# Last gates ahead of last rows, residual on VectorE, first mixer re-dealt, and unread identity products on TensorE

## The chip, the cores and the metric

The kernel runs on one core of one Trainium2 chip. The metric is the device time of one execution in microseconds (us), from the host's side of the launch to its end; the traces give the span from the first to the last instruction. All engines work at once and meet through semaphores: TensorE (PE in the rows, its weight loads PEld), VectorE (DVE), ScalarE (ACT), GpSimd (POOL) and SyncE (SP), which issues the weight transfers.

## What is computed

Two blocks of two layers each, on 256 tokens of 1024 values in fp32. In each layer a swiglu feed-forward (FFN) stands on either side of a mixer. Block 1 normalises by root mean square, and its mixer has four branches, merged by gates; block 2 normalises by mean and variance after each part, and its mixer has two branches.

```python
# block 1, one layer
f = swiglu(rms_norm(h, g0), w_gate, w_up, w_down)      # 1024 -> 2816 -> 1024
h = h + 0.5 * rms_norm(f, g0_post)
a.., b.., c_q, c_k, c_v, d_q, d_k, d_v, d_f, gates = split(rms_norm(h, g1) @ w_in)
y_a = short_conv(...) @ w;  y_b = conv_31_layernorm_silu(...) @ w
y_c = rms_norm(differential_attention(c_q, c_k, c_v)) @ w
y_d = forgetting_attention(d_q, d_k, d_v, d_f) @ w
h = h + rms_norm((g_a*y_a + g_b*y_b + g_c*y_c + g_d*y_d) @ w_o, g1_post)
# then a second FFN like the first
# block 2, one layer (DN = 4 ** 0.25)
x = layernorm(DN * x + 0.5 * swiglu_2(x, w13, w2), g, b)
qa, ka, va, qkv_b, beta, dt, z, gates = split(x @ w_in)
y_a = sliding_window_attention(qa, ka, va, bias, sink) @ w_branch_a      # 16 heads
q, k, v = split(silu(conv_4(qkv_b)))
y_b = (rms(gated_delta_rule(l2(q), l2(k), v, g(dt), beta)) * silu(z)) @ w_branch_b   # 8 heads
x = layernorm(DN * x + (g_a * y_a + g_b * y_b) @ w_out, g, b)
# then a second FFN like the first
```

## The kernel before

**Products.** Every weight matrix comes from `stream` in units of up to 1 MB, by SP's queue, into a ring of four slots (`weight_ring`). ACT rounds a unit to a high part (L1537) and VectorE takes the low part as the difference (L1862); in block 2's mixer GpSimd takes it (L908) for the units of projections and gates. Each product of weights is then three products of parts on TensorE (high by high, low by high, high by low).

**Order.** `plan_first` and `plan_second` write a list of steps for one layer of each block, and every engine walks the same list and runs its own handler of each step, so the list is the order on every queue. A step that uses a weight unit draws in the splits of units that come later, ahead of its own work. `plan_ffn` deals an FFN: 22 steps `gu` (TensorE L1044, gate and up for 128 hidden values, whose silu is ACT's L1578 and whose split into parts VectorE's L1869 and L1871) and 11 steps `down` (L1101, of which each reads the hidden values of two `gu`). `interleave` weaves a chain of small dependent steps (attention, delta rule) into rounds of dense projection work and pops the steps that follow a finished projection from the list `later`, one for each step of the chain.

**Ends of the parts.** After the last rows (`last_rows`, L1112) ACT sums squares (block 1, `post`, L1585) or VectorE takes statistics (block 2, `post2`, L2150 to L2161), GpSimd computes the reciprocal root (L865, L867), and VectorE builds a diagonal (L1856) or the normed rows (L2161). TensorE then turns the rows for the next part (`xt`: L1061, fp32 products with the diagonal, in block 1; L1063, transposes, in block 2) into the PSUM banks 6, 7, 4 and 5. The sum of an FFN stands in the banks 0 to 3, that of a mixer in 4 to 7; VectorE reads bank 6, which holds the second half of the tokens, as the third of the four (L1939 or L2150).

**Mixer of block 1.** The chain is attention c (L1242 scores, L1257 turns, L1286 values), then its `out_norm`: squares by ACT (L1671), the root by GpSimd (L865, L867), the scaling by VectorE (L2105); then `out_turn`, and attention d. The gates are TensorE's L1346 with L1349 for the branch value, merged by VectorE's L2126.

**Mixer of block 2.** `pk`, `ps`, `pq` and `pv` project keys, small logits, queries and values. `cumg` (VectorE L2203, ACT L1746) sums the decays. For the eight heads of the delta rule `dtr` (TensorE L1402) turns queries and keys after the convolution (VectorE `taps` L2230 and L2232, `silu` L2245), `ddc` (L1428) and `dkk` build the decay matrix, and steps `dl0` to `du4` and `dot` solve two heads at a time. `affine` (GpSimd L935 and L937, in each of the three parts of a layer) makes the residual from the normed rows by gain and bias, four operations of 1024 columns.

## Time and profile before

| | |
|---|---|
| median of 3 runs | 3339.35 us (3338.19 to 3339.7) |
| profiled execution | 3333.8 us, span 3332.1 us, mean granted TensorE clock 0.959 |
| TensorE busy | 3070.4 us (92%) |
| VectorE, ScalarE, GpSimd busy | 1944.3, 1341.5, 532.0 us |
| block 1: FFN, mixer, FFN of layer 0 | 15 to 213, 219 to 572, 578 to 774 us |
| block 2: FFN, mixer, FFN of layer 0 | 1549 to 1770, 1772 to 2239, 2242 to 2441 us |

Layer 1 of each block repeats the pattern (784 to 1541 and 2446 to 3318 us). A row of the trace has the start in us, the duration in us (for several instructions from the first's start to the last's end), the engine, the line, the operation with its tiles, and in brackets the idle time of the engine ahead of it with what ended it. A row of the windows gives for a stretch the busy time of each engine with the count of its instructions, and then PEclk, the TensorE clock that was granted as a share of full speed: 1.00 is 2.4 GHz and 0.50 is 1.2 GHz.

### The profile page before, as it was taken

The numbers are of one execution on the slowest core, as the hardware profiler recorded it, in microseconds if no ns is written. First come the engines' busy times: TensorE is split into PE (matmuls) and PEld (weight loads), VectorE is DVE, ScalarE is ACT, GpSimd is POOL, SyncE is SP. The second block draws the span as 40 slices with busy tenths as digits, with TensorE's granted clock in tenths as the row PEclk, the third lists the DMA queues.
The fourth block names the chain that finished last, engine by engine and source line by source line (L and its number), as shares of the span: only waits on it lengthen the run. The fifth ranks groups of instructions, "written<-read, shape, count | busy, mean of one in ns | idle before, by whom it ended". The sixth has DMA issues, their size and how long they took to land.

```text
span 3332.1 us, 59102 instructions
## 1 busy us (share of the span) xinstructions
PE 3070.4 (92%) x22178; PEld 2901.9 (87%) x22178; DVE 1944.3 (58%) x3310; ACT 1341.5 (40%) x2224; POOL 532.0 (16%) x471
## 2 busy tenths in 40 slices
PE   8989999998989999998898978989989998889998
PEld 7989898998989999897797877989979888789897
DVE  4556776555556876554554576466565536654755
ACT  4344454434344454432333534434333345433332
POOL 0000000000000000001103444431010044444300
PEclk9999999999999999998898999999999989999999
DMA  5544444554544445456552321255545422123453
GB/s 207 182 159 153 132 144 168 176 188 148 189 158 154 142 142 171 165 186 150 198 202 102 102 77 54 87 177 181 190 162 200 160 100 89 64 66 138 170 188 127
DMA packets 72442, 495.49 MB, mean 149 GB/s; under 512 B 8064, under 2 KB 8240, under 8 KB 20176
## 3 DMA queue, kind: packets, MB, share of 16 engines
q1 hardware_dynamic: 67824, 471.95, 41.5%
q0 software_dynamic: 4048, 18.59, 2.1%
q8 instruction: 184, 3.01, 0.4%
q14 instruction: 114, 0.93, 0.1%
q10 hardware_dynamic: 272, 0.99, 0.1%
HBM read 487.31 MB, written 4.19 MB: 148 GB/s over the span
## 4 chain that ended last, share of the span: by engine, by line
issue 74%; PE 12%; DVE 6%; POOL 4%; POOLq 2%; DVEq 2%; ACT 1%; DMA 0%; ACTq 0%; SPq 0%
PE psum L1132 4%; POOL weights_low L908 2%; DVE work L2232 1%; PE psum L1346 1%; PE psum L1352 1%; POOL small L867 1%; POOLq L936 1%; PE psum L1242 1%; POOL residual L937 1%; POOLq L866 1%; DVE small L2257 0%; PE psum L1188 0%; DVE work L2318 0%; PE psum L1457 0%; DVEq L2235 0%
## 5 line engine op out<-in xcount | busy, mean ns | idle before, releaser
L1537 ACT ACTIVATE weights_high<-weight_ring 128x2048 fp32r<-128x2048 f32 (+3 forms) x788 | 906.8, 1171 | 1105.0 <-DMA weight_ring<-stream 1097.6
L1862 DVE TENSOR_TENSOR weights_low<-weight_ring,weights_high 128x2048 fp32r<-128x2048 f32 (+6 forms) x532 | 906.6, 1710 | 757.3 <-ACT weights_high L1537 753.8
L1044 PE MATMUL psum<-normed_t_high,weights_high 128*128 128x256 f32 x2816 | 802.5, 285 | 11.6 <-DVE normed_t_low L1871 10.5
L1044 PE MATMUL psum<-normed_t_low,weights_high 128*128 128x256 f32 x2816 | 800.2, 284 | 0.0
L1044 PE MATMUL psum<-normed_t_high,weights_low 128*128 128x256 f32 x2816 | 799.6, 284 | 0.0
L1044 PEld LDWEIGHTS psum<-normed_t_high,weights_high 128*128 128x128 f32 x2816 | 542.9, 193 | 17.4 <-DVE normed_t_low L1871 11.8
L1044 PEld LDWEIGHTS psum<-normed_t_low,weights_high 128*128 128x128 f32 x2816 | 543.9, 193 | 3.6
L1044 PEld LDWEIGHTS psum<-normed_t_high,weights_low 128*128 128x128 f32 x2816 | 543.6, 193 | 0.0
L1101 PE MATMUL psum<-weights_high,work_parts 128*128 128x512 f32 x1472 | 464.5, 397 | 19.5 <-DVE work_parts L1871 19.5
L1132 PE MATMUL psum<-normed_t_high,weights_high 128*128 128x256 f32 x1248 | 394.8, 316 | 3.2 <-DVE normed_t_low L1871 2.1
L908 POOL TENSOR_TENSOR weights_low<-weight_ring,weights_high 128x512 fp32r<-128x512 f32 (+1 forms) x216 | 346.2, 1618 | 274.6 <-ACT weights_high L1537 274.6
L1132 PE MATMUL psum<-normed_t_low,weights_high 128*128 128x256 f32 x1248 | 361.3, 290 | 0.0
L1132 PE MATMUL psum<-normed_t_high,weights_low 128*128 128x256 f32 x1248 | 360.7, 289 | 0.0
L865 POOL TENSOR_TENSOR small<-small 128x1 f32<-128x1 f32 (+3 forms) x74 | 18.9, 256 | 2107.5 <-ACT work L1585 992.6
L1101 PEld LDWEIGHTS psum<-weights_high,work_parts 128*128 128x128 f32 x1472 | 271.0, 189 | 77.8 <-DVE work_parts L1871 19.9
L1101 PE MATMUL psum<-weights_low,work_parts 128*128 128x512 f32 x736 | 290.9, 395 | 0.0
L1132 PEld LDWEIGHTS psum<-normed_t_high,weights_high 128*128 128x128 f32 x1248 | 248.0, 199 | 17.4 <-issue 11.3
L1346 PE MATMUL psum<-normed_t_high,weights_high 128*128 128x256 f32 x768 | 236.5, 308 | 14.8 <-DVE weights_low L1862 9.4
L1132 PEld LDWEIGHTS psum<-normed_t_low,weights_high 128*128 128x128 f32 x1248 | 248.5, 199 | 1.1
L1132 PEld LDWEIGHTS psum<-normed_t_high,weights_low 128*128 128x128 f32 x1248 | 247.0, 198 | 0.0
L1346 PE MATMUL psum<-normed_t_low,weights_high 128*128 128x256 f32 x768 | 222.5, 290 | 0.0
L1346 PE MATMUL psum<-normed_t_high,weights_low 128*128 128x256 f32 x768 | 222.2, 289 | 0.0
(268 smaller groups left out, 4477.5 us busy)
## 6 DMA issues: line engine op xcount, KB each, us to landing
weight_ring<-stream SPq DMA_DIRECT2D x400, 1024.0 KB, 4.9
weight_ring<-stream SPq DMA_DIRECT2D x64, 768.0 KB, 4.2
feature_rows<-feat POOLq DMA_DIRECT2D x6, 1024.0 KB, 5.1
work<-toeplitz_rows POOLq DMA_DIRECT2D x8, 512.0 KB, 6.6
feature_rows<-feat POOLq DMA_DIRECT2D x6, 512.0 KB, 3.8
toeplitz_rows<-work POOLq DMA_DIRECT2D x1, 3072.0 KB, 36.4
params<-prms POOLq DMA_DIRECT2D x5, 251.5 KB, 3.3
residual<-x SPq DMA_DIRECT2D x2, 512.0 KB, 4.3
```

Of the source, the lines that this page charges most:

```text
L866: pool.drain()
L867: pool.tensor_tensor(dst, dst, HALFNEG[:, 0:dst.shape[1]], ALU.pow).then_inc(signal, 1)
L908: pool.tensor_tensor(some(LOW, i, q, n), some(RING, i, q, n), some(HIGH, i, q, n).bitcast(F32), ALU.subtract).then_inc(low_by_pool, n)
L936: pool.drain()
L937: pool.tensor_tensor(H[:, t, :], H[:, t, :], PG[:, 1, :], ALU.add).then_inc(residual_ready, 1)
L1044: ins = pe.matmul(PS[:, bank, at:at + S], w[a][:, first + k, c * P:(c + 1) * P], src[b][:, k, :], start=(k, m) == (0, 0), stop=(k, m) == ( ...
L1101: ins = pe.matmul(PS[:, b, :], src[c][:, r, t * P:(t + 1) * P], w[a][:, r, n * HALF:(n + 1) * HALF], start=start and m == 0, stop=False, s ...
L1132: ins = pe.matmul(PS[:, job.bank, c * S:(c + 1) * S], w[i][:, k, c * P:(c + 1) * P], XT[j][:, k, :], start=(k, m) == (0, 0), stop=(k, m) = ...
L1242: ins = pe.matmul(dst, q[:, t * P:(t + 1) * P], k[:, 0:keys], start=True, stop=not extra, skip_group_check=True)
L1346: ins = pe.matmul(PS[:, job.bank, 0:S], w[p][:, r, 0:P], XT[q][:, r, :], start=(r, m) == (0, 0), stop=(r, m) == (KB - 1, 2), skip_group_ch ...
L1537: return act.activation(dst, src, ACT.Copy, scale=scale)
L1862: dve.tensor_tensor(some(LOW, i, q, n), some(RING, i, q, n), some(HIGH, i, q, n).bitcast(F32), ALU.subtract).then_inc(low_by_vector, n)
```

## The change

- `plan_ffn`: the last `gu` step goes ahead of the next-to-last `down`, so the end is gu20, gu21, down9, down10 where it was gu20, down9, gu21, down10. All eight FFNs.
- Ends of both mixers: before, the eight last gates and the rows steps ran 24 25, 26 27, wo0, 28 29, wo1, 30 31, wo2, wo3; now 24 to 27, 28 29, wo0, 30 31, wo1, wo2, wo3 (block 2: gates 0 to 7 likewise).
- Mixer of block 1: a step `out_square` (squares and root) follows attention c at once; the scaling comes three chain steps later and the turn after one more. The projections `dv` move behind those of branch a.
- Block 2: `affine` goes from GpSimd to VectorE, in four quarters of two operations of 512 columns, at gu4, gu6, gu8, gu10 of an FFN and after `pk`, the two `pq` and `pv` of a mixer. `feature` (the load of gains on GpSimd's queue) comes at gu12. `post2` drops its wait for the residual, and VectorE waits once for GpSimd's memsets ahead of block 2.
- Mixer of block 2: `cumg` moves into the attention; `taps` becomes single steps of one tap, and `interleave` pops two steps where more than four stand in `later`; the order in `prepare` changes; the scaling of `du4` becomes a step `dsc`; gates shift between the pairs of heads, so that the last pair has three dense units instead of four.
- `warm`: ahead of each wait for normed rows in `xt`, except at a layer's first `xt`, TensorE multiplies the identity by itself (fp32, 128 x 128) into the last quarter of the first `xt` bank: 24 and 4 products in block 1, 12 and 8 in block 2. Nothing reads them. The wait for the first bank stands ahead of them.

```diff
+WARM = {1: (24, 4), 2: (12, 8)}
...
@@ -178,11 +179,12 @@
     for j in range(FB):
         pl.step("gu", ("gu", s, j), banks=["hi"], s=s, j=j, unit=("gu", s, j),
                 signals=[("gate_silu_ready", 1), ("hidden_ready", 1)])
-        if j >= 2 and j % 2 == 0:
+        if 2 <= j < FB - 2 and j % 2 == 0:
             down(j // 2 - 1)
         for kind, signals, args in after:
             if j in args["j"]:
                 pl.step(kind, signals=signals, s=s, j=j, p=args["j"].index(j))
+    down(FP - 2)
     down(FP - 1)
...
         f()
-        if later:
-            later.pop(0)()
+        for _ in range(2 if len(later) > 4 else 1):
+            if later:
+                later.pop(0)()
...
-    chain.append((3, lambda: pl.step("out_norm", ("on", "c"), br="c",
-                                     signals=[("out_squares_summed", 1), ("out_rsqrt_ready", 1)])))
-    chain.append((2, out_turn("c")))
+    squares = (1, lambda: pl.step("out_square", "out_square",
+                                  signals=[("out_squares_summed", 1), ("out_rsqrt_ready", 1)]))
+    out_norm = (1, lambda: pl.step("out_norm", ("on", "c"), br="c"))
...
-    chain += chain_d[:8]
+    chain += [squares] + chain_d[:2] + [out_norm] + chain_d[2:3] + [(2, out_turn("c"))] + chain_d[3:8]
...
-    chain += [(2, lambda: pl.step("out_norm", ("on", "d"), br="d",
-                                  signals=[("out_squares_summed", 0), ("out_rsqrt_ready", 0)])),
-              (2, out_turn("d"))]
-    dense = [(16, lambda what=what, p=p: project(what, p)) for what in ("dq", "dk", "dv") for p in range(2)]
+    chain += [(2, lambda: pl.step("out_norm", ("on", "d"), br="d")), (2, out_turn("d"))]
+    dense = [(16, lambda what=what, p=p: project(what, p)) for what in ("dq", "dk") for p in range(2)]
     dense += [(16, lambda p=p: gate_a(p)) for p in range(4)] + [(16, lambda p=p: value_a(p)) for p in range(2)]
+    dense += [(16, lambda p=p: project("dv", p)) for p in range(2)]
     dense += [(12, lambda j=j: gate(j)) for j in range(24)]
     interleave(pl, chain, dense)
-    pl.steps += [gate(24)[0], gate(25)[0]]
+    pl.steps += [gate(j)[0] for j in range(24, 28)]
     acc = pl.step("acc", ("acc", 1), banks=acc_hi, s=1)
-    for k in range(2, KB + 1, 2):
-        if k < KB:
-            pl.steps += [gate(24 + k)[0], gate(24 + k + 1)[0]]
-        pl.step("wo", ("wo", k // 2 - 1), k=k // 2 - 1, unit=("wo", k // 2 - 1), src=("gy", 24 + k - 2))
+
+    def wo(k):
+        pl.step("wo", ("wo", k), k=k, unit=("wo", k), src=("gy", 24 + 2 * k))
+
+    pl.steps += [gate(j)[0] for j in range(28, 30)]
+    wo(0)
+    pl.steps += [gate(j)[0] for j in range(30, 32)]
+    for k in range(1, 4):
+        wo(k)
...
-        pl.step("affine", ("affine", s), s=s, signals=[("residual_ready", 2)])
         if s == 2:
             pl.step("params", signals=[("params_loaded", 16)])
-        if s != 1:
-            pl.step("feature", signals=[("feature_rows_loaded", 16)], s=s)
-        else:
+        if s == 1:
             pl.step("small_split", signals=[("small_weights_ready", 1)])
             pl.step("factors")
+
+    def affine(s, p):
+        pl.step("affine", s=s, p=p, signals=[("residual_ready", 1)])
 
     def post(s, acc):
         pl.step("post2", ("post", s), s=s, acc=acc,
@@ -375,7 +382,11 @@
     def ffn(s):
         begin(s)
         acc = pl.step("acc", ("acc", s), banks=acc_lo, s=s)
-        plan_ffn(pl, s, [("bias", [("bias_loaded", 16)], {"j": (3, 7, 11, 15)})] if s == 0 else [])
+        beside = [("affine", [("residual_ready", 1)], {"j": (4, 6, 8, 10)}),
+                  ("feature", [("feature_rows_loaded", 16)], {"j": (12,)})]
+        if s == 0:
+            beside.append(("bias", [("bias_loaded", 16)], {"j": (3, 7, 11, 15)}))
+        plan_ffn(pl, s, beside)
...
-        return host, [lambda: pl.step("taps", ("taps", hp, w, 0), hp=hp, w=w, p=0,
...
+        rest = []
+        for c in range(2):
+            for n in range(3):
+                rest.append(lambda c=c, n=n: pl.step("tap", hp=hp, w=w, p=c, a=n))
+            rest.append(lambda c=c: pl.step("taps", ("taps", hp, w, c), hp=hp, w=w, p=c, a=3,
+                                            signals=[("conv_ready", 1), ("conv_tanh_ready", 1)]))
+        rest.append(lambda: pl.step("silu", ("silu", hp, w), hp=hp, w=w, signals=[("conv_silu_ready", 1)]))
+        return host, rest
...
     pl.step("pk", "pk", banks=["lo"], unit=("w", 4))
+    affine(1, 0)
     pl.step("ps", "ps", banks=["lo"],
             signals=[("small_proj_ready", 1), ("small_logs_ready", 1), ("log_decay_ready", 1)])
     for p in range(2):
         pl.steps.append(query(p)[0])
+        affine(1, 1 + p)
     pl.step("pv", "pv", banks=["lo"], unit=("w", 5))
-    pl.step("cumg", "cumg", banks=["s"],
-            signals=[("decay_diff_ready", 1), ("decay_exps_ready", 1), ("decay_scalars_ready", 1)])
+    affine(1, 3)
...
+        for h, b in zip(hs, banks):
+            add(h, "dtr", b, [("qk_squares_summed", 1), ("qk_rsqrt_ready", 1)])
+            add(h, "dte", [], [("head_scalars_ready", 1)])
+        for h, b in zip(hs, banks):
+            add(h, "ddc", [3], [("decay_ready", 1), ("strict_decay_ready", 1)])
+            add(h, "dtf", b)
+        for h in hs:
+            add(h, "dkk", [3], [("level_masked", 1)])
+        return steps
...
+        for h in hs:
+            steps.append(lambda h=h: pl.step("dsc", ("dsc", h), h=h))
...
+    steps.insert(9, (2, lambda: pl.step("cumg", "cumg", banks=["s"],
+                                        signals=[("decay_diff_ready", 1), ("decay_exps_ready", 1),
+                                                 ("decay_scalars_ready", 1)])))
+    first = [(4, f) for f in prepare((0, 1), ((6, 7), (4, 5)))]
+    chain = steps + first[:1] + last + first[1:]
     dense = [(16, lambda p=p: query(p)) for p in (2, 3)] + [(16, lambda w=w: conv(0, w)) for w in range(3)]
     dense += [(16, lambda p=p: gated(p)) for p in range(2)] + [(16, lambda w=w: conv(1, w)) for w in range(3)]
+    dense += [(16, lambda: gate(0, 0, "lo3"))]
     interleave(pl, chain, dense)
...
-    extra = [[(16, lambda: gate(0, 0, "lo3"))] + [(16, lambda w=w: conv(2, w)) for w in range(3)],
-             [(16, lambda: gate(0, 1, "lo3"))] + [(16, lambda w=w: conv(3, w)) for w in range(3)],
-             [(16, lambda p=p: gated(p)) for p in (2, 3)] + [(16, lambda k=k: gate(0, k, "lo3")) for k in (2, 3)],
-             [(16, lambda k=k: gate(0, k, "lo3")) for k in range(4, 8)]]
+    extra = [[(16, lambda w=w: conv(2, w)) for w in range(3)] + [(16, lambda: gate(0, 1, "lo3"))],
+             [(16, lambda w=w: conv(3, w)) for w in range(3)] + [(16, lambda: gated(2))],
+             [(16, lambda: gated(3))] + [(16, lambda k=k: gate(0, k, "lo3")) for k in range(2, 5)],
+             [(16, lambda k=k: gate(0, k, "lo3")) for k in range(5, 8)]]
     for hp in range(pairs):
         chain = [(2, f) for f in solve((2 * hp, 2 * hp + 1))]
         if hp + 1 < pairs:
-            todo = [f for h in (2 * hp + 2, 2 * hp + 3) for f in prepare(h, (6, 7, 3))]
-            for n, f in enumerate(todo):
-                chain.insert(2 + 3 * n, (2, f))
+            todo = [(2, f) for f in prepare((2 * hp + 2, 2 * hp + 3), ((6, 7), (6, 7)))]
+            ends = chain[-4:]
+            chain = chain[:-4]
+            for n, item in enumerate(todo[:8]):
+                chain.insert(2 + 4 * n, item)
+            chain += todo[8:] + ends
         interleave(pl, chain, extra[hp])
...
+    pl.steps += [gate(1, k)[0] for k in range(4)]
...
+            def warm(bank, n):
+
+                for _ in range(n):
+                    pe.matmul(PS[:, bank, HALF - P:HALF], IDENT, IDENT, start=True, stop=True, skip_group_check=True)
+
             def xt(st):
                 flush()
 
                 n = named(("norm", st.s)).at["normed_ready"] if now.blk == 1 else 2 * st.s
-                for t in range(T):
+                first = st.jobs[0]
+                pe.wait_ge(bank_taken[first.bank], turn_at(first))
+                for t in range(T):
+                    warm(first.bank, WARM[now.blk][t] if st.s else 0)
                     pe.wait_ge(normed_ready, reach("normed_ready", n - 1 + t))
                     for k in range(KB):
                         job = st.jobs[k // 2]
-                        if t == 0 and k % 2 == 0:
+                        if t == 0 and k and k % 2 == 0:
...
+            def affine(st):
+
+                if st.p == 0:
+                    dve.wait_ge(feature_rows_loaded, reach("feature_rows_loaded", 16 * st.s))
+                t, cols = st.p // 2, slice(st.p % 2 * HALF, (st.p % 2 + 1) * HALF)
+                dve.tensor_tensor(H[:, t, cols], XN[:, t, cols], PG[:, 0, cols], ALU.mult)
+                dve.drain()
+                dve.tensor_tensor(H[:, t, cols], H[:, t, cols], PG[:, 1, cols], ALU.add).then_inc(residual_ready, 1)
+                dve.drain()
...
                 def stats(t, n):
                     job = st.acc.jobs[2 * t + n]
                     cols = slice(n * HALF, (n + 1) * HALF)
-                    if n == 0:
-                        dve.wait_ge(residual_ready, reach("residual_ready", 2 * (st.s + 1) - 1 + t))
...
             dve.tensor_copy(XN[:, :, :], H[:, :, :]).then_inc(normed_ready, T)
+            dve.wait_ge(zeros_set, 3)
```

How the order of instructions moves at three places. TensorE between the last rows of the first FFN of block 1 and the turn of the normed rows (line numbers of each kernel; `constants` is the identity), before:

```order
L1112 MATMUL psum<-weights_low,work_parts 128x512
L1054 REGISTER_ALU
L1058 REGISTER_ALU
L1061 MATMUL psum<-work,residual 128x128 x4
L1058 REGISTER_ALU
L1061 MATMUL psum<-work,residual 128x128 x2
```

And now:

```order
L1138 MATMUL psum<-weights_low,work_parts 128x512
L1077 REGISTER_ALU
L1070 MATMUL psum<-constants 128x128 x24
L1080 REGISTER_ALU
L1087 MATMUL psum<-work,residual 128x128 x4
L1084 REGISTER_ALU
L1087 MATMUL psum<-work,residual 128x128 x2
```

Twenty-four products of the identity stand between the last rows and the first turn; four more (L1070 x4) stand between the two halves of the tokens.

VectorE in the mixer of block 1 about the scaling of attention c (L2105, L2129 after), with the taps of branch b (L1979, L2003) and the gate's merge (L2126, L2150), before:

```order
L2126 SCALAR_TENSOR_TENSOR work<-work,psum 128x256
L2105 TENSOR_TENSOR work<-psum,small 128x512 x2
L1861 REGISTER_ALU
L1862 TENSOR_TENSOR weights_low<-weight_ring,weights_high 128x768
L2124 REGISTER_ALU
L2126 SCALAR_TENSOR_TENSOR work<-work,psum 128x256
```

And now:

```order
L2150 SCALAR_TENSOR_TENSOR work<-work,psum 128x256
L2003 SCALAR_TENSOR_TENSOR work<-work 128x232 x2
L1885 REGISTER_ALU
L1886 TENSOR_TENSOR weights_low<-weight_ring,weights_high 128x768
L2129 TENSOR_TENSOR work<-psum,small 128x512 x2
L1885 REGISTER_ALU
L1886 TENSOR_TENSOR weights_low<-weight_ring,weights_high 128x384
```

The scaling now stands behind a pair of taps and a low split, some 37 instructions of VectorE later in the layer.

VectorE in the mixer of block 2 at the first convolution (`taps`; L2230 and L2232 are L2264 and L2265 after), before:

```order
L2230 TENSOR_SCALAR work<-psum,params 128x256
L2232 SCALAR_TENSOR_TENSOR work<-psum,params,work 128x255
L2232 SCALAR_TENSOR_TENSOR work<-psum,params,work 128x254
L2232 SCALAR_TENSOR_TENSOR work<-psum,params,work 128x253
L2230 TENSOR_SCALAR work<-psum,params 128x256
L2232 SCALAR_TENSOR_TENSOR work<-psum,params,work 128x255
```

And now, at the second:

```order
L2264 TENSOR_SCALAR work<-psum,params 128x256
L2265 SCALAR_TENSOR_TENSOR work<-psum,params,work 128x255
L2110 REGISTER_ALU
L2113 REGISTER_ALU
L2116 TENSOR_TENSOR small<-small 128x16
L2118 RECIPROCAL small<-small 128x16
L2129 TENSOR_TENSOR work<-psum,small 128x512 x2
L2265 SCALAR_TENSOR_TENSOR work<-psum,params,work 128x254
```

Steps of the chain now stand between the taps of one convolution, where before its eight operations stood in one piece.

## Rows read from the trace of the kernel before

**Rows 1.** The page: TensorE's busy time, its share of the span, its instructions.

```profile
PE 3070.4 (92%) x22178; PEld 2901.9 (87%) x22178; DVE 1944.3 (58%) x3310; ACT 1341.5 (40%) x2224; POOL 532.0 (16%) x471
```

**Rows 2.** TensorE's waits: waiting line, releaser: us in total, times, longest.

```profile
PE psum L1061 <- DVE work L1856: 48.3, 6, 16.0
PE psum L1402 <- DVE work L2245: 31.6, 6, 5.5
...
PE psum L1112 <- DVE work_parts L1871: 18.5, 10, 2.0
...
PE psum L1257 <- ACT work L1650: 9.2, 2, 4.6
```

**Rows 3.** Timeline: the first last-rows wait of an FFN.

```profile
207.22 0.73 PE L1112 MATMUL psum<-weights_high,work_parts 128*128 128x512 f32 x2 [1.82 <-DVE work_parts L1871]
```

**Rows 4.** Windows: behind such a wait, then behind one of block 1's mixer.

```profile
769.00:772.50 3.50, 3.50 (x10) 2.75 (x9) 0.00 (x0) 0.00 (x0) 0.00 (x0) 0.52 0.58 173
376.50:383.50 7.00, 6.19 (x29) 6.20 (x30) 6.70 (x14) 2.84 (x6) 0.00 (x0) 0.51 0.27 74
```

**Rows 5.** Timeline of block 1's mixer, TensorE, then VectorE.

```profile
377.31 0.79 PE L1349 MATMUL psum<-work_parts,weights_high 128*128 128x256 f32 x2 [3.43 <-DVE work_parts L1871]
...
404.56 0.57 PE L1346 MATMUL psum<-normed_t_high,weights_high 128*128 128x256 f32 x1 [4.02 <-DVE weights_low L1862]
...
402.27 1.29 DVE L2105 TENSOR_TENSOR work<-psum,small 128x512 f32<-128x512 f32 x2 [5.07 <-POOL small L867]
```

**Rows 6.** Timeline of block 2's first FFN, VectorE and GpSimd.

```profile
1588.75 3.81 DVE L1862 TENSOR_TENSOR weights_low<-weight_ring,weights_high 128x2048 fp32r<-128x2048 f32 x1 [21.56 <-ACT weights_high L1537]
...
1595.00 2.54 DVE L1871 TENSOR_TENSOR work_parts<-work,work_parts 128x256 fp32r<-128x256 f32 x1
1597.46 2.28 DVE L1862 TENSOR_TENSOR weights_low<-weight_ring,weights_high 128x2048 fp32r<-128x2048 f32 x1
...
1590.38 4.40 POOL L935 TENSOR_TENSOR residual<-work,feature_rows 128x1024 f32<-128x1024 f32 x1
```

**Rows 7.** Timeline of block 2's mixer, VectorE, GpSimd and TensorE.

```profile
1816.42 4.38 DVE L2203 TENSOR_TENSOR small<-small 128x16 f32<-128x16 f32 x1
...
1816.23 4.54 POOL L908 TENSOR_TENSOR weights_low<-weight_ring,weights_high 128x2048 fp32r<-128x2048 f32 x1 [1.02 <-ACT weights_high L1537]
...
1919.00 0.86 PE L1428 MATMUL psum<-work,constants 128*128 128x256 f32 x2 [2.65 <-DVE work L2291]
...
2000.36 0.90 PE L1402 MATMUL psum<-constants,work 128*128 128x128 f32 x3 [5.11 <-DVE work L2245]
```

**Rows 8.** Windows of block 2's mixer: after two waits, and ahead of a third.

```profile
1823.50:1831.00 7.50, 7.19 (x30) 6.32 (x31) 0.93 (x7) 3.46 (x15) 0.00 (x0) 0.54 0.00 0
1997.50:2005.00 7.50, 4.64 (x24) 4.64 (x24) 3.73 (x12) 3.33 (x13) 1.11 (x2) 0.54 0.03 12
1902.50:1935.30 32.80, 24.57 (x182) 23.57 (x180) 28.95 (x68) 15.53 (x42) 17.95 (x17) 0.91 0.35 125
```

**Rows 9.** Timeline about three waits for normed rows, TensorE, then VectorE.

```profile
219.15 1.22 PE L1061 MATMUL psum<-work,residual 128*128 128x128 f32 x4 [6.07 <-DVE work L1856]
...
577.67 1.64 PE L1061 MATMUL psum<-work,residual 128*128 128x128 f32 x6 [5.90 <-DVE work L1856]
...
2242.27 1.40 PE L1063 MATMUL psum<-constants,work 128*128 128x128 f32 x8 [3.57 <-DVE work L2161]
...
574.62 1.41 DVE L1939 SCALAR_TENSOR_TENSOR work<-psum,small,feature_rows 128x512 f32<-128x512 f32 x2 [0.78 <-POOL small L867]
...
2239.95 0.69 DVE L2150 SCALAR_TENSOR_TENSOR work<-psum,residual 128x512 f32<-128x512 f32 x1
```

**Rows 10.** Windows: fp32 products of 128 x 128 at either clock, then block 2's second `xt`.

```profile
219.15:222.70 3.55, 3.55 (x16) 3.55 (x17) 0.29 (x1) 0.85 (x2) 1.33 (x3) 0.50 0.02 8
581.40:583.30 1.90, 1.86 (x17) 1.67 (x15) 0.41 (x2) 1.28 (x4) 0.00 (x0) 1.00 0.00 0
1772.50:1783.00 10.50, 7.55 (x34) 6.44 (x31) 6.35 (x12) 5.57 (x9) 0.74 (x2) 0.51 0.16 69
```

121 lines of the change are left out of this document (49 added, 72 removed).

## Prediction

> **What bounds the kernel now.** I read the page first: TensorE is busy for 92% of the span [rows 1], so a gain is either a wait of TensorE or a stretch in which it works at half clock. Next its waits [rows 2]: they name who ends each, and they are short and many. Then, for each edit, the timeline at the place [rows 3, 5, 6, 7, 9] and the windows behind a wait [rows 4, 8, 10], since several waits are followed by some 3.5 to 7 us at a granted clock of 0.5, in which TensorE's busy time counts double. Each gain below is therefore the idle time plus half of the busy time in the half-clock stretch behind it. One core, so a saved microsecond on TensorE is one of the span unless another engine is then late.
>
> **1. Last gates ahead of last rows.** Ten waits of last rows for VectorE's hidden parts cost 18.5 us, the longest 2.0 [rows 2]: eight FFN ends of 1.8 to 1.9 (the first is 1.82 [rows 3]), some 15 in all, and two mixer ends with the other 3.6. In the new order the rows step that comes first reads hidden values that are one step older, and the step that needs the last ones has a whole rows step in front of it. All 18.5 go. Behind the second FFN's wait the clock was 0.52 for 3.5 us [rows 4], which gives 1.75; I take 1.5 for the mixer's that is like it. In block 2's first FFNs VectorE's next splits, which ran ahead of the first statistics, now come nearer to them: 1.8 off in two layers. Sum 20, bounds 15 and 22.
>
> **2. Mixer of block 1.** GpSimd's root stands behind eight squares by ACT, VectorE waits 5.07 us for it ahead of L2105 and holds a low split behind that, and TensorE's gate waits 4.02 for that split [rows 5]. The other wait, 3.43 at L1349, is for the branch value of a, whose last operation on VectorE is just in time for nothing [rows 5]. The change separates the scaling from its root by about 37 VectorE instructions, and the convolution of a comes two units ahead of its first gate. Half clock behind it: 6.19 us busy at 0.51 [rows 4], 3.1 regained; I take 2.9 for the stretch like it behind the other. With 4.02 and 3.43, and up to 0.7 of short waits, 14.1 a layer, 28.2 in two. But VectorE had no gap ahead of the L1349 wait, and the splits it owes do not become fewer; up to 2 us a layer may come back as a wait for low splits. I take 24, bounds 12 and 28.
>
> **3. Residual to VectorE, block 2's first FFN.** A low split of 2048 columns took 3.81 us beside GpSimd's L935 and L937 (4.40 for one of them) [rows 6], where the next such split took 2.28; the cast and the low part between them were held too, 2.54 us for the second of 256 columns. TensorE stood for all of that. 1.5 for the split and nearly two for each of the small ones make some 5.1 that go; VectorE's new wait for GpSimd's memsets gives up to 1.6 back. I take 3.5, bounds 0 and 6. Elsewhere in FFNs eight operations of 512 columns, about 0.7 us each by L2150's 0.69 [rows 9], lie on a VectorE that is busy 58% of the span [rows 1], between gu steps whose weight splits are done a unit ahead: nothing. In the mixer they are put ahead of attention, where VectorE had gaps: nothing, but see the rivals.
>
> These rows show VectorE held by GpSimd: L2203, 16 columns, took 4.38 us beside a GpSimd split of 4.54 that began 0.19 earlier [rows 7]. The Trainium skill has a rule for it ("SBUF — State Buffer", SBUF: two separate sides): the two engines share one pair of ports, and whichever starts first holds it for its whole instruction, where VectorE's operation reads two inputs from SBUF. The trace agrees. By that rule the new residual operations, which read two SBUF inputs, can each be held for one GpSimd split in the mixer; it is the slower rival's mechanism.
>
> **4. Mixer of block 2, two layers.** Idle, from [rows 2, 7]: 4.6 a layer at L1257, where attention begins behind `cumg`, itself held as just said; 2.65 at L1428; and 31.6 in both layers at L1402, six waits of which the three of a layer are alike (5.11 is one), because VectorE runs eight taps and the silu in one piece ahead of what the turn needs. That is 4.6 + 2.65 + 15.8 = 23.0 a layer. `cumg` inside the attention leaves dense rounds beside it; single taps let chain steps pass; L1428 now has a turn of the other head before it. I let half of the first L1402 wait stay (2.6), since VectorE was busy for 28.95 of the 32.8 us ahead of it [rows 8] and order alone cannot shorten that. 20.4. Half clock: five stretches a layer stand behind these waits, 7.19 and 4.64 us busy in two of them [rows 8], some 22.5 us busy in all five, so 11.3 lost; two thirds come back with the waits, 7.5. The short waits in the solving steps (up to 1.7 each) I leave. 28 a layer, 56 in two. Bounds: 25, if VectorE is the limit all through; 80, if the short waits go too.
>
> **5. Unread products.** Price: eight fp32 products (two records each) took 3.55 us at half clock, and eight to nine 1.86 at full [rows 10]: 0.24 and 0.45 each. They gain only where they end before the rows are ready.
> - Block 1, after the first FFN: TensorE idles 6.07 us [rows 9], bank 6 is free, 24 products need 5.8 at full clock. The turns then run at 1.0 in place of 0.5 (3.55 to 1.9), four more products take 1.0 of that. Gain 0.7, twice.
> - Block 1, after the mixer: the products wait for bank 6, which VectorE frees with the first half of L1939 at 574.62, so at 575.35. 24 products from there, the first at half clock, end at about 583; the turns began at 577.67 [rows 9] and ended at 583.3. With turns and four more products the end comes to 587.5 to 588. Loss 4.7, twice: 9.4.
> - Block 2, after the first FFN: twelve (2.9) and eight (1.9) fit about the two waits; gain 0.4, twice. After the mixer bank 6 is read at 2239.95, twelve products end at 2243.6, 1.3 after the 2242.27 at which turns began [rows 9]. Loss 1.2, twice.
> - Clock behind block 2's turns: 7.55 us busy at 0.51 [rows 10], of which the dense products after the turns are 4.4, so 2.2 a place, a little more after the mixer; 9.6 in four if the clock stays up. What came before was an engine idle for half of the time, now filled, but the turns between are short: I take half, 4.8.
>
> Of these turns the rows show that the clock of 0.51 outlasts eight transposes and rises only well into the products [rows 10]. The Trainium skill ("TensorE: Matmul & The Clock Gate", Part 4: PE-mode transpose) says that transposes do not count as busy for the clock; with it alone block 2's gain would be the full 9.6 or nothing, by whether the unread products suffice.
>
> Net: 1.4 − 9.4 + 0.8 − 2.4 + 4.8 = −4.8, bounds −16 and +8.
>
> **Sum.** 20 + 24 + 3.5 + 56 − 4.8 = 98.7. Every part is read as if nothing new were late; of the 80 us in the two mixers I take a tenth off for that. 90 us from the profiled execution's 3333.8 is 3244; the median lies 5.6 above that execution, which gives 3249.
>
> **Rivals.**
> - A. VectorE is the limit in block 2's mixer: the waits for it move, 25 of 56 stay. For it: 28.95 of 32.8 busy [rows 8]; against: it is busy 58% on the whole, and after the other three pairs' waits much is slack. 3249 + 31 = 3280. Chance 0.2.
> - B. The unread products cost nothing, and no new waits come: + 5 and + 9, with the full mixer of block 1, + 4: 3231. For it: the post's products could be hidden if the clock stays high from the rows on. Against: bank 6's date in [rows 9]. Chance 0.2.
> - C. Slower: the residual's eight operations in block 2's mixer are each held by a GpSimd split, 4.5 us apiece by [rows 7], 36 a layer, and stand ahead of the first score on VectorE's queue. It decides when the last quarter is not done by the time at which scores begin; from there each microsecond is TensorE's, and part 4 is lost as well: 3249 + 72 + 56 = 3377. Against: there is a gap of 1.02 us between GpSimd's splits [rows 7] in which VectorE gets in, and only one of each quarter's two can be caught by the same split. Chance 0.04.
> - D. It does not do what it says: the unread products don't hold the clock, and block 1's places cost more, with the waits of part 1 only moved. 3249 + 12 + 10 = 3271. Chance 0.11.
>
> **Numbers.** Forecast 3249 with chance 0.45 for within some 12 us of it. The range 3212 to 3298 takes in A, B and D and the upper bound of part 4; it leaves C out and A with part 2's low end. Faster by over 0.2% (about what a measurement of this kernel can tell from no change) 0.93, within 0.02, slower 0.05.
>
> **What would show it.** Right: no L1112 wait over 0.5 us, none at L1257, a mixer of block 2 shorter by 25 to 30 us, VectorE's L2129 free of a long wait for GpSimd; after both mixers of block 1 the first turn 4 to 5 us later, measured from the last rows. Wrong: low-split waits on the gates of block 1, residual operations of 4 us in block 2's mixer, the L1402 successor still waiting 5 us in each pair.

## The result, and the profile after

The changed kernel takes 3300.36 us (median; 3299.18 to 3302.04) where the kernel before took 3338.77 beside it: a ratio of 0.9889 with a 95% interval of 0.9871 to 0.9906. It is faster by 38 us (31 to 43), where 90 were forecast. The sign was right, the size was not, and the time lies outside the range of 3212 to 3298.

The page of the changed kernel, its span and its busy times, to be held against [rows 1]:

```profile
span 3298.1 us, 59917 instructions
## 1 busy us (share of the span) xinstructions
PE 3095.6 (94%) x22562; PEld 2932.6 (89%) x22562; DVE 1934.7 (59%) x3364; ACT 1339.5 (41%) x2214; POOL 463.7 (14%) x445
```

The span is 34.0 us shorter, but TensorE is busy for 25 us more. The two traces can be split into three terms: TensorE's idle time, half of its busy time in the stretches that the trace has at a granted clock of 0.5 (what the half clock costs), and the rest, its work as if at full clock.

| trace | span | idle | cost of half clock | work at full clock |
|---|---|---|---|---|
| before | 3332.1 | 261.8 | 94.3 | 2976.0 |
| after | 3298.1 | 202.4 | 78.4 | 3017.2 |
| difference | -34.0 | -59.4 | -15.9 | +41.2 |

The 41 us of new work are the 192 unread products (28 at four places of block 1, 20 at four of block 2): at 0.234 us each they are 45. So the idle time fell by 59 us, but most of that was filled, not removed.

TensorE's waits, in the columns of [rows 2] (lines shift by some 26 to 46: L1070 is the unread product, L1283 the turn in attention, L1428 the turn of a head, L1454 the decay product, L1534 the turn of a head's scaled output, which the expectations call the product by the scaled output):

```profile
PE psum L1087 <- DVE work L1880: 23.9, 3, 15.4
PE psum L1534 <- DVE work L2361: 14.4, 8, 2.1
PE psum L1127 <- DVE work_parts L1895: 13.2, 1, 13.2
PE psum L1483 <- DVE work L2352: 12.9, 10, 2.1
PE psum L1454 <- DVE work L2309: 12.3, 2, 6.1
...
PE psum L1175 <- DVE weights_low L1886: 9.5, 2, 4.7
PE psum L1428 <- DVE work L2279: 9.3, 2, 4.6
...
PE psum L1283 <- ACT work L1676: 7.3, 2, 3.7
PE psum L1070 <- DVE work L1963: 7.3, 2, 3.7
```

The last-rows wait of 18.5 us (L1112 before) is gone from the list, the 48.3 at the turns of block 1 became 23.9, and the head turns' 31.6 became 9.3. L1175 and L1070 are new. Three others were there before and grew: L1483 from 11.2 us (L1457), L1534 from 8.8 (L1508, twice as many and half as long), L1454 from 5.3 (L1428). The kernel before had for these:

```profile
PE psum L1457 <- DVE work L2318: 11.2, 10, 1.6
PE psum L1508 <- DVE work L2326: 8.8, 16, 1.1
PE psum L1428 <- DVE work L2291: 5.3, 2, 2.7
```

Where the 34 us are, by stage, worked out from the two timelines. A stage runs from the end of one part's last rows (the start of the first turn, or of the first unread product, less the idle time in its brackets) to the end of the next part's (the last row ends with the last rows of the kernel); the two layers are added:

| stage, both layers | before | after | difference |
|---|---|---|---|
| block 1, first FFNs | 418.6 | 413.5 | -5.1 |
| block 1, mixers | 715.1 | 702.7 | -12.4 |
| block 1, second FFNs | 408.6 | 409.8 | +1.2 |
| block 2, first FFNs | 433.0 | 424.1 | -8.9 |
| block 2, mixers | 937.6 | 930.3 | -7.3 |
| block 2, second FFNs | 405.9 | 404.4 | -1.5 |

The stretch from last rows to the first product of the next part is inside these: in block 1 12.2 to 11.5 after the FFN and 12.1 to 15.7 after the mixer, in block 2 8.7 to 10.3 after the FFN and 10.1 to 12.0 after the mixer (first layers).

### The profile page after: what moved, and what is told of

It reads as the page before. It is cut to its first block, busy times and chain, and to the rows that moved or that the text cites. A ratio compares the mean times of both kernels' runs of the same rounds, so it can differ in the third digit from the quotient of the medians.

```text
span 3298.1 us, 59917 instructions
## 1 busy us (share of the span) xinstructions
PE 3095.6 (94%) x22562; PEld 2932.6 (89%) x22562; DVE 1934.7 (59%) x3364; ACT 1339.5 (41%) x2214; POOL 463.7 (14%) x445
## 3 DMA queue, kind: packets, MB, share of 16 engines
HBM read 487.31 MB, written 4.19 MB: 149 GB/s over the span
## 4 chain that ended last, share of the span: by engine, by line
issue 67%; PE 22%; DVE 5%; POOL 2%; DVEq 2%; POOLq 1%; ACT 1%; DMA 1%; ACTq 0%; SPq 0%
PE psum L1158 5%; PE psum L1062 4%; PE psum L1372 2%; PE psum L1127 2%; PE psum L1378 2%; POOL weights_low L940 1%; PE psum L1070 1%; PE psum L1268 1%; POOL small L899 1%; DMA weight_ring<-stream 1%; PE psum L1495 1%; DVE work L2265 1%; POOLq L898 1%; PE psum L1493 0%; PE psum L1483 0%
## 5 line engine op out<-in xcount | busy, mean ns | idle before, releaser
L1563 ACT ACTIVATE weights_high<-weight_ring 128x2048 fp32r<-128x2048 f32 (+5 forms) x778 | 906.2, 1184 | 1122.0 <-DMA weight_ring<-stream 1114.6
L1886 DVE TENSOR_TENSOR weights_low<-weight_ring,weights_high 128x2048 fp32r<-128x2048 f32 (+4 forms) x538 | 886.9, 1655 | 781.9 <-ACT weights_high L1563 778.9
L940 POOL TENSOR_TENSOR weights_low<-weight_ring,weights_high 128x512 fp32r<-128x512 f32 (+2 forms) x214 | 349.5, 1649 | 287.2 <-ACT weights_high L1563 286.8
```

The lines of the kernel that those rows point to most:

```text
L940: pool.tensor_tensor(some(LOW, i, q, n), some(RING, i, q, n), some(HIGH, i, q, n).bitcast(F32), ALU.subtract).then_inc(low_by_pool, n)
L1563: return act.activation(dst, src, ACT.Copy, scale=scale)
L1886: dve.tensor_tensor(some(LOW, i, q, n), some(RING, i, q, n), some(HIGH, i, q, n).bitcast(F32), ALU.subtract).then_inc(low_by_vector, n)
```

## Experiments

Each time is the median of four to twelve executions. Medians from different sets of runs can differ by 2 to 3 us without meaning (the kernel before came out between 3338.8 and 3341.4), and ratios have intervals of 0.0010 to 0.0022 to either side. Where a stage is named it is from the profile, by the rule above, first and second layer. A profile is of one execution, and not always of a typical one: that of the kernel without unread products took 3290.0 us where its median is 3284.4, that of block 2's order undone 3326.6 (median 3319.1), that of the new FFN ends alone 3323.5 (median 3317.5).

**No unread products.**

```diff
-WARM = {1: (24, 4), 2: (12, 8)}
+WARM = {1: (0, 0), 2: (0, 0)}
```

> The changed kernel with no unread products (both counts zero); the wait for the first bank stays. Theory 1: the products delay the first turn after the four mixers and help nowhere else, so the stretches from last rows to first product shrink by what they grew (3.5 in block 1 after the mixer, 1.9 in block 2 after the mixer, 1.5 in block 2 after the FFN, less the 0.7 gained in block 1 after the FFN, all twice): 3288 us. Theory 2: the products also keep the clock up behind block 2's turns (no stretch at 0.5 there in the changed kernel, where one of 10.5 us stood before), and the 1.5 after block 2's FFN is late rows, not products: 7 gained in block 1 after the mixer, 1.5 lost after the FFN, some 7 lost in block 2, 3302 us, as the changed kernel.

3284.37 us (3280.76 to 3289.98), ratio 0.9829 (0.9812 to 0.9847): 16 us faster without the products by the medians, 10 by the two traces. The difference of 6 between the two is that the traced execution was the longest of its five (3289.98, the others 3280.8 to 3284.8) and had the lowest mean granted clock (0.959, the others 0.960 to 0.962). Theory 1 holds for the sum. In block 1 the stage behind the mixer went back from 204.2 and 205.6 to 200.9 and 202.2. But theory 2 was right on the clock. The windows over the turns and first products behind block 2's first FFN, of this kernel and then of the changed one (columns as in [rows 4]):

```profile
1745.00:1757.00 12.00, 9.29 (x46) 8.43 (x47) 7.83 (x17) 7.05 (x10) 0.74 (x2) 0.57 0.01 4
```

```profile
1750.00:1762.00 12.00, 8.34 (x62) 7.30 (x63) 8.08 (x18) 7.05 (x10) 0.74 (x2) 1.00 0.04 16
```

With the products the clock is 1.00 throughout, without them 0.57. All eight places say the same, each over the 12 us from its last rows: without products 0.62 to 0.72, with them 1.00 behind the four first FFNs and 0.86 behind the four mixers. Theory 2 was right on the rows too: without products block 2's first product comes 10.8 us after the first FFN's last rows, so they are not what moved it from 8.7 to 10.3. They do what they are there for, but at a price: between the two traces they add 47 us of work, fill 21 us of idle time and save 17 us of half clock, and 10 are left over.

**The unread products in another bank.**

```diff
-                first = st.jobs[0]
-                pe.wait_ge(bank_taken[first.bank], turn_at(first))
+                spare = st.jobs[2 if st.s == 2 else 0]
+                pe.wait_ge(bank_taken[spare.bank], turn_at(spare))
...
-                    warm(first.bank, WARM[now.blk][t] if st.s else 0)
+                    warm(spare.bank, WARM[now.blk][t] if st.s else 0)
...
```

> The changed kernel with the unread products behind a mixer written to the third bank of the turn (bank 4, which VectorE reads first) in place of the first (bank 6, read third). Theory: the bank's date is the whole cost: TensorE's wait of 3.65 us ahead of the first product falls to under 1, the first turn comes when the rows are ready, and from last rows to first product block 1 needs 11.5 us in place of 15.7, block 2 some 10.5 in place of 12; twice each, 11 us in all: 3289. Rival: the first rows are late anyway and the clock falls in the wait for the rows of the second half, so that under 4 us come: 3297 or more.

3282.84 us (3280.1 to 3285.61), ratio 0.9829 (0.9811 to 0.9846): 17.5 us, more than the whole 11 of the theory. Behind block 1's mixer the changed kernel, then this one:

```profile
566.65 6.96 PE L1070 MATMUL psum<-constants 128*128 128x128 f32 x48 [3.65 <-DVE work L1963]
573.46 1.95 PE L1087 MATMUL psum<-work,residual 128*128 128x128 f32 x16
```

```profile
560.32 5.62 PE L1070 MATMUL psum<-constants 128*128 128x128 f32 x48 [0.24 <-DVE work L1963]
565.98 2.05 PE L1087 MATMUL psum<-work,residual 128*128 128x128 f32 x16
```

In bank 6 TensorE waits 3.65 us, drops to half clock in it (24 products take 6.96 us), and the turns come 10.5 us after the last rows; in bank 4 it waits 0.24, the 24 products take 5.62, and the turns come at 5.9, when the rows are ready. The 12 us from the last rows are now granted 1.00 at all eight places. The bank's date was the cost.

**The order inside block 2's mixer undone.** `prepare`, `extra`, the place of `cumg`, the tap steps and the scaling as before; residual on VectorE, ends and unread products as changed.

```diff
-        for _ in range(2 if len(later) > 4 else 1):
-            if later:
-                later.pop(0)()
+        if later:
+            later.pop(0)()
...
+    first = [prepare(0, (6, 7, 3)), prepare(1, (4, 5, 3))]
+    chain = steps + [(4, first[0][0])] + last + [(4, f) for f in first[0][1:2] + first[1][:1] + first[0][2:4]
+                                               + first[1][1:2] + first[0][4:] + first[1][2:]]
...
```

> The changed kernel with the order of before inside block 2's mixer (decay sums ahead of attention, four taps in a piece, one step popped, head preparation, scaling and gates as before); the residual on VectorE, the ends and the unread products stay. Theory: shorter waits of 2 us, each with 3.5 us of half clock, took the place of the long ones, and the first preparation waits longer than before, so that the re-deal is worth 0 to 5 us: 3300 to 3305. Rival 1: it is worth the 16 us by which TensorE's idle time fell in the two mixers: 3316. Rival 2: it is worth the predicted 56, and something else took them: 3356.

3319.08 us (3314.27 to 3326.6), ratio 0.9934 (0.9917 to 0.9950): the re-deal is worth 19 us, near rival 1; my theory of 0 to 5 fell. I had taken the stages, 468.8 us a layer before and 466.0 and 464.3 after, as the worth. But with the old order in the new surroundings the mixer takes 475.9 and 475.6 (in the longest of six executions): some 7 us a layer are lost by what stands around it (1.5 of it the later first product). I had read a difference of two stages as the worth of one edit.

**The order inside block 1's mixer undone.** Squares, scaling and turn in one place, `dv` ahead of branch a.

```diff
+    chain += [(3, norm_c), (2, out_turn("c"))]
...
-    chain += [squares] + chain_d[:2] + [out_norm] + chain_d[2:3] + [(2, out_turn("c"))] + chain_d[3:8]
+    chain += chain_d[:8]
...
```

> The changed kernel with the order of before inside block 1's mixer (squares, scaling and turn of attention c in one place, value projections of d ahead of branch a); the mixer's end stays as changed. Theory: the wait for low splits of 4.73 us that the changed kernel shows behind branch a replaces the 3.43 of before, and only the 4.0 us behind the scaling with its half clock were won, less short waits elsewhere: 4 to 8 us for two layers, 3304 to 3308. Rival: the re-deal is worth the predicted 24: 3324.

3297.72 us (3297.55 to 3298.55), ratio 0.9873 (0.9853 to 0.9893): no slower than the changed kernel, so neither figure came. In its own stage the re-deal is worth 7 us (354.0 and 355.8 undone, 352.6 and 350.1 changed). But block 2's mixer, whose code this edit doesn't touch, took 459.9 and 457.4 in place of 466.0 and 464.3, with the same waits. That the medians agree (block 1's mixers are 7 us slower and the whole is not) says that this is not one odd execution. It was the first sight of the effect that the two runs with added products test.

**GpSimd's splits in quarters.**

```diff
-                    pool.wait_ge(high_ready, reach("high_ready", QUARTERS * i + q + n))
-                    pool.tensor_tensor(some(LOW, i, q, n), some(RING, i, q, n), some(HIGH, i, q, n).bitcast(F32),
-                                       ALU.subtract).then_inc(low_by_pool, n)
+                    for r in range(q, q + n):
+                        pool.wait_ge(high_ready, reach("high_ready", QUARTERS * i + r + 1))
+                        pool.tensor_tensor(some(LOW, i, r, 1), some(RING, i, r, 1), some(HIGH, i, r, 1).bitcast(F32),
+                                           ALU.subtract).then_inc(low_by_pool, 1)
```

> The changed kernel with GpSimd's low splits of whole units (2048 columns, 4.6 us) issued as four of 512 columns. Theory: at the start of block 2's attention the scores wait because GpSimd's split holds VectorE's operation on two columns for 4.19 us, so that the decay sums, which were moved away, were only the victim; in quarters the hold is at most 1.3 us, TensorE's 3.61 us wait there falls under 1 us and the half clock behind it (9.1 us busy) goes: 5 to 7 us a layer, 3288. Rival: ScalarE's table load and the length of the score chain set that start, and under 3 us come in all: 3298.

3282.38 us (3278.46 to 3288.17), ratio 0.9832 (0.9819 to 0.9846): 18 us, more than the 10 to 14 of the theory. The start of attention in the changed kernel:

```profile
1794.10 4.19 DVE L2074 TENSOR_SCALAR small<-small 128x2 f32<-128x2 f32 x1
...
1793.75 4.52 POOL L940 TENSOR_TENSOR weights_low<-weight_ring,weights_high 128x2048 fp32r<-128x2048 f32 x1 [0.80 <-ACT weights_high L1563]
...
1799.44 0.90 PE L1283 MATMUL psum<-constants,work 128*128 128x128 f32 x3 [3.61 <-ACT work L1676]
```

And with quarters:

```profile
1794.08 0.91 DVE L2075 TENSOR_SCALAR small<-small 128x2 f32<-128x2 f32 x1
...
1796.53 0.55 PE L1284 MATMUL psum<-constants,work 128*128 128x128 f32 x3 [0.72 <-ACT work L1677]
```

With `cumg` away, GpSimd's split of 4.52 us held another small operation for 4.19: the same hold as in [rows 7] with another victim. In quarters it is 0.91 and TensorE's wait falls from 3.61 to 0.72. Behind the wait of 3.61 the clock was 0.50 from 1798.3 to 1808.6 with 9.16 us busy, and behind the one of 0.72 it was 1.00 from 1796 to 1806. Of the 17 us between the two traces only 3.5 are idle time and 14 are half clock; 9 of the 14 are these stretches in two layers, and the other 5 stand elsewhere, where the alignment described below could give them too. That the hold lasts as long as GpSimd's instruction is what the Trainium skill says ("SBUF — State Buffer", SBUF: two separate sides); the trace agrees at both lengths.

**The decay matrix ahead of head 1's scalars.**

```diff
-    first = [(4, f) for f in prepare((0, 1), ((6, 7), (4, 5)))]
+    first = prepare((0, 1), ((6, 7), (4, 5)))
+    first = [(4, first[n]) for n in (0, 1, 2, 4, 5, 3, 8, 6, 7, 9)]
```

> The changed kernel with the first pair's preparation in the order of before (decay matrix of head 0 ahead of head 1's scalars). Theory: in the changed order VectorE's decay step of head 0 stands behind head 1's scalars, which wait for squares on ScalarE and the root on GpSimd, and TensorE waits 6.13 us for the bank; the old order brings 2.7 again, 7 us for two layers: 3293. Rival: VectorE is the limit through the whole preparation, the wait moves to the turns of the next pair, and the time stays: 3300.

3291.14 us (3288.22 to 3291.92), ratio 0.9855 (0.9839 to 0.9871): 9 us, and the wait of 6.13 us is gone (1.7 stand in its place). Mixers 462.1 and 460.7. The rival is right in a part: three waits of 1.5 to 1.7 us stand near by instead, and the next turn's wait rose from 4.63 to

```profile
1919.47 1.54 PE L1429 MATMUL psum<-constants,work 128*128 128x128 f32 x6 [5.20 <-DVE work L2280]
```

**The value projections of d ahead of branch a.**

```diff
-    dense = [(16, lambda what=what, p=p: project(what, p)) for what in ("dq", "dk") for p in range(2)]
+    dense = [(16, lambda what=what, p=p: project(what, p)) for what in ("dq", "dk", "dv") for p in range(2)]
```

> The changed kernel with the value projections of branch d ahead of branch a again; squares and scaling of attention c stay apart. Theory: VectorE's work for branch a is a backlog that some wait pays for, the 4.73 us for low splits goes and the 3.43 us for the branch value comes back, each with 3.5 to 7 us of half clock: 3300, within 3. Rival: the move of the projections alone is what costs, and its undoing brings the half clock too: 3292.

3293.37 us (3290.98 to 3295.06), ratio 0.9866 (0.9851 to 0.9882). In block 1's mixer two waits of 2.32 (for low splits) and 2.34 us (for the branch value) replace the one of 4.73, which is the backlog that the theory said: the sum is 4.66. Its stage gained 2.2 us in one layer and none in the other; the rest of the 7 lies in block 2's mixer again (462.4 and 460.7).

**The kernel before with the new FFN ends alone.**

```diff
-        if j >= 2 and j % 2 == 0:
+        if 2 <= j < FB - 2 and j % 2 == 0:
...
+    down(FP - 2)
     down(FP - 1)
```

> The kernel before with the new end of the eight FFNs alone (the last gates step ahead of the next-to-last rows). Theory: eight waits of 1.8 to 1.9 us go with the half clock that stood behind one of them, and nothing else moves: 17 to 19 us, 3321. Rival 1: the statistics of block 2 come later by VectorE's splits and give half back: 3330. Rival 2: shorter gaps save more clock than the stretches show, since TensorE idles less ahead of each turn: over 25 us, under 3314.

3317.53 us (3313.06 to 3323.51), ratio 0.9936 (0.9922 to 0.9950): 21 us (17 to 26), as expected to within its spread. Rival 1 is seen in the trace, though: block 2's first product comes 10.4 us after the FFN's last rows in place of 8.7, and block 2's mixers, whose order is still the old one, take 473.9 and 470.5 us in place of 468.8.

**Four mends together, and a fifth.** The four are the bank, the quarters, the decay matrix and `dv`; the fifth takes the scaling ahead of the masks:

```diff
-            ends = chain[-4:]
-            chain = chain[:-4]
+            ends = chain[-2:]
+            chain = chain[:-2]
```

> The changed kernel with four mends at once: unread products behind a mixer in bank 4, GpSimd's low splits in quarters, the decay matrix ahead of head 1's scalars, the value projections of d ahead of branch a. Alone they gave 17.5, 18.0, 9.2 and 7.0 us. Theory: they act at places apart, but the last two gave part of theirs through the alignment of half-clock stretches in block 2's mixer, which a sum counts twice: 38 to 46 us, 3254 to 3262. Rival 1: they add up, 3249. Rival 2: one shared cause (less half clock by luck of alignment) stood behind most of it, 3275.

3262.35 us (3260.05 to 3266.68), ratio 0.9769 (0.9752 to 0.9785). 38 us below the changed kernel, the lower edge of the theory: alone they gave 52. It is the fastest kernel here, 2.3% below the kernel before. The traces, each less that of the changed kernel and split as above, say which part doesn't add up:

| mend | idle | cost of half clock | work |
|---|---|---|---|
| bank 4 | -10.6 | -10.7 | +2.2 |
| quarters | -3.5 | -14.1 | +1.0 |
| decay matrix first | -5.8 | -1.8 | -0.1 |
| `dv` first | -0.9 | -8.9 | +1.1 |
| sum of the four | -20.8 | -35.5 | +4.2 |
| the four together | -20.8 | -19.5 | +3.8 |

The idle times add up to the tenth; the half clock gives little more than half of its sum. So the parts of the four that were half clock are not theirs alone.

> The changed kernel with the scaling of a pair's two heads ahead of the next pair's level masks, not behind them, in the three pairs that prepare another. Theory: the waits of 2.07, 2.05 and 1.62 us at the product by the scaled output come from VectorE's order (the scaling, whose root is ready 4 us before, stands behind two masks, one of them held by GpSimd); they go, with up to 1.7 us of half clock behind each: 12 to 18 us for two layers, 3285. Rival: VectorE then waits for the root ahead of the masks and the first solving step of the next pair waits instead: 3300.

3298.27 us (3297.04 to 3300.13), ratio 0.9875 (0.9857 to 0.9893): the rival. The waits, of the changed kernel above 14.4 in eight:

```profile
PE psum L1472 <- DVE work L2368: 10.7, 12, 1.3
...
PE psum L1534 <- DVE work L2361: 2.9, 2, 1.5
```

L1534 lost 11.5 us, and L1472, the first solving product of the next pair, gained 10.7: it now waits for L2368, VectorE's merge of the output by its gate, which this order brings ahead of it. VectorE has two things to do for TensorE at the same time, and either order makes TensorE wait for the other.

> The four mends and the scaling ahead of the masks. Theory: the fifth brings here what it brings alone, 12 us or more below the kernel with four. Rival: with fewer waits before it the clock is up already, and it brings its idle time only, 8 to 11 us.

3265.63 us (3262.32 to 3266.99), ratio 0.9777 (0.9762 to 0.9793): nothing gained over four, which the run of the fifth alone says too; both figures of mine were wrong.

**The kernel before with quarters alone, and quarters with the decay sums put back.**

The first has the same edit as above in the kernel before.

> The kernel before with GpSimd's low splits in quarters and nothing else. Theory: the wait of 4.58 us at the start of block 2's attention is the hold, whoever is the victim, so it goes here too although the decay sums stand where they stood, with 3.3 us of half clock: 13 to 18 us, 3324. Rival: here the decay sums' own chain (VectorE, ScalarE) sets the start and the quarters bring under 5 us: 3335.

3333.18 us (3329.2 to 3339.57, twelve runs), ratio 0.9983 (0.9973 to 0.9993): 6 us by the ratio and 8 by the medians, so between the two, nearer to the rival's under 5. The wait did fall, from 4.58 to 2.01 us, but the mixers of block 2 took 468.3 and 471.5 us and were no shorter.

```diff
+    pl.step("cumg", "cumg", banks=["s"],
+            signals=[("decay_diff_ready", 1), ("decay_exps_ready", 1), ("decay_scalars_ready", 1)])
...
-    steps.insert(9, (2, lambda: pl.step("cumg", "cumg", banks=["s"],
...
```

> The changed kernel with GpSimd's splits in quarters and the decay sums ahead of attention again. Theory: hold and decay sums both stand in front of the first turn, so either one alone brings little; with the hold broken TensorE waits some 2 us there (2.01 in the kernel before with quarters) in place of 0.7, with a half-clock stretch, and the kernel is 4 to 8 us slower than with quarters alone (3282.4): 3288. Rival: the hold was all, and the place of the sums makes no difference: 3282.

3291.82 us (3286.84 to 3296.47), ratio 0.9855 (0.9832 to 0.9878): 9 us slower than with quarters alone. Between the two traces 2 us of that are idle time and 10 are half clock, so the time alone is a weak measure of the place of the sums; the wait is a better one. TensorE's wait at the first turn in the four cases, this kernel's row being

```profile
1797.06 0.89 PE L1283 MATMUL psum<-constants,work 128*128 128x128 f32 x3 [2.22 <-ACT work L1676]
```

| wait at attention's first turn, us | whole splits | quarters |
|---|---|---|
| decay sums ahead | 4.58 (before) | 2.01 (before with quarters), 2.22 |
| decay sums inside | 3.61 (changed) | 0.72 |

Each edit alone takes 1.0 or 2.6 us of the 4.6; together they take 3.9. Two causes stood side by side in front of one wait.

**More unread products, as a delay.**

```diff
-WARM = {1: (24, 4), 2: (12, 8)}
+WARM = {1: (28, 4), 2: (12, 8)}
```

> The changed kernel with 28 in place of 24 unread products ahead of the first turn in block 1: four places of 4 x 0.24 us, a delay of 3.8 us in all by the end of block 1 and the same code behind it. Theory (alignment): a wait of 2 us costs a half-clock stretch or not by where it falls, so block 2's mixer, with the same idle time of 46 us a layer, comes out at 457 to 466 us a layer in another pattern, and the whole differs from 3300.4 + 3.8 = 3304 by 3 us or more. Rival: the clock follows the idle time alone, the mixers stay at 466 and 464, and the whole is 3304.

> As the one with 28, but 31: a delay of 6.7 us. Theory (alignment): the mixers of block 2 come out at another value than with 24 or 28, 457 to 466. Rival: 3307 and mixers of 466 and 464.

With 28: 3295.66 us (3295.01 to 3301.78), ratio 0.9875 (0.9853 to 0.9897). With 31: 3303.31 (3297.64 to 3306.32), ratio 0.9891 (0.9872 to 0.9910). Neither differs from the changed kernel beyond its interval, so the times alone settle nothing; but block 2's mixers, with the same code and 46 us of idle time, took 463.6 and 460.9, and 463.5 and 460.9, in place of 466.0 and 464.3. The run with 31 came out as that with 28, not at another value. What differs is the half clock alone. The stages of this mixer in the four kernels that have the same code there, each less its idle time and less half of its busy time at half clock:

| kernel | stage | idle | busy at half clock | what is left |
|---|---|---|---|---|
| changed | 466.0, 464.3 | 46.5, 46.4 | 49.0, 45.7 | 394.9, 395.1 |
| with 28 | 463.6, 460.9 | 46.0, 46.3 | 45.4, 39.2 | 394.9, 395.0 |
| with 31 | 463.5, 460.9 | 46.2, 46.5 | 45.7, 38.3 | 394.5, 395.3 |
| block 1's order undone | 459.9, 457.5 | 45.3, 45.3 | 39.3, 34.3 | 395.0, 395.0 |

How that can be is seen where the same wait falls twice. The turn of the scaled output in the changed kernel, for the first pair and for the second, and the windows behind them:

```profile
1979.10 0.64 PE L1534 MATMUL psum<-constants,work 128*128 128x128 f32 x2 [2.07 <-DVE work L2361]
...
2039.57 0.44 PE L1534 MATMUL psum<-constants,work 128*128 128x128 f32 x2 [2.05 <-DVE work L2361]
```

```profile
1979.00:1983.00 4.00, 3.90 (x20) 3.90 (x21) 3.34 (x11) 0.87 (x2) 0.00 (x0) 0.57 0.00 0
2039.50:2043.50 4.00, 3.93 (x23) 3.93 (x24) 3.65 (x12) 1.11 (x2) 0.00 (x0) 0.64 0.01 4
```

And the second pair's, the same product behind the same wait, in the kernel with block 1's order undone:

```profile
2047.35 0.44 PE L1536 MATMUL psum<-constants,work 128*128 128x128 f32 x2 [2.05 <-DVE work L2363]
```

```profile
2047.00:2051.00 4.00, 3.65 (x32) 3.66 (x33) 3.66 (x12) 1.12 (x2) 0.00 (x0) 1.00 0.16 27
```

Behind 2.05 us of idle time the same product had a window at 0.64 with 23 products in one kernel and one at 1.00 with 32 in the other, though in the 5 us ahead of the wait TensorE was busy for 4.57 us at 1.00 in both. A wait of 2 us costs 2 or nearly 4. I call this alignment, since only the time at which the wait falls differs here; what in that time decides, these runs don't show.

**Four mends without unread products.**

> The kernel with four mends and no unread products. Theory: with the bank free in time the products bring the 0.7 to 1.2 us of each first turn in block 1 (four places) and the clock behind block 2's turns: 3268, 5 us above the kernel with them (3262.4). Rival: they bring nothing, as the change of 1.5 us between no products and products in bank 4 suggests: 3262 to 3264.

3272.02 us (3269.54 to 3274.94), ratio 0.9797 (0.9779 to 0.9815): 10 us slower than with them. With the bank free in time the products pay, more than I thought; with the original bank they cost 16. The 10 us hold for the kernel with all mends: in the changed kernel products in bank 4 and no products at all are 1.5 us apart (3282.84 and 3284.37), which is nothing.

## Why the prediction was wrong

**Part 1 (20) was right in its places.** The ends of the eight FFNs alone bring 21 us (17 to 26), where the forecast had some 15 for them, and no last-rows wait over 0.5 us is left. The ends of the two mixers, with the other 5, were not tried alone. The shift of block 2's statistics was under-sized: 1.7 us a layer to the first product in place of 0.9.

**Part 2 (24) was over by 17: by the stages it is worth 7, under its lower bound of 12.** The scaling did leave its wait: 4.02 us are gone. The step that failed is "up to 2 us a layer may come back as a wait for low splits". What came back is 4.73 a layer:

```profile
368.06 0.57 PE L1175 MATMUL psum<-weights_high,normed_t_high 128*128 128x256 f32 x1 [4.73 <-DVE weights_low L1886]
```

With smaller ones the waits inside the mixer come to 8.5 us, where they were 8.1. VectorE had no gap ahead of the old wait of 3.43, which I had written down and then charged at 2; it came back in full and more. What was gained is half clock: two stretches with 12.1 us busy became one with 3.4.

**Part 3 (3.5) was right in kind, low in size.** The wait behind the transfer fell by 6.3 us. Before and after:

```profile
PE psum L1101 <- DVE work_parts L1871: 19.5, 1, 19.5
```

```profile
1576.34 1.22 PE L1127 MATMUL psum<-weights_high,work_parts 128*128 128x512 f32 x2 [13.21 <-DVE work_parts L1895]
```

Its stage is 6.7 us shorter (220.2) than where only the FFN's end was changed (226.9); that is a difference of stages, for the move of the residual was not undone alone. This was outside the bounds too (0 and 6). Of rival C the mechanism came and the price did not: two of the eight residual operations in each mixer of block 2 were held for some 5 us, but the last was done 6 us before the first score (1792.25).

```profile
1779.08 4.93 DVE L2171 TENSOR_TENSOR residual<-work,feature_rows 128x512 f32<-128x512 f32 x1
...
1785.64 0.69 DVE L2173 TENSOR_TENSOR residual<-residual,feature_rows 128x512 f32<-128x512 f32 x1
```

**Part 4 (56) failed; it is worth 19.** This is the largest miss, 37 of the 52 us, and it lies under the lower bound of 25. Four steps of it:
- "4.6 a layer at L1257, where attention begins behind `cumg`, itself held": I named the hold and then costed the edit as though the victim were the cause. The hold stayed with another victim, and 3.61 of the 4.58 us of wait stayed with it. Breaking the hold takes it to 0.72.
- "L1428 now has a turn of the other head before it": what it has in front of it on VectorE is head 1's scalars, and those wait for ScalarE's squares and GpSimd's root. The wait rose from 2.65 to 6.13 (L1454 after); undoing that order brings 9 us. I had read TensorE's order and not VectorE's.
- Half of the first head turn's wait was to go: 5.19 became 4.63. VectorE is the limit there, as rival A says.
- The two long waits of the later pairs went (5.11 and 5.47), but four of 1.5 to 2.1 came at L1534 and two of 2.1 at L1483. The idle time of a mixer fell from 54.5 to 46.4 us, 8 where 20 were forecast. And the clock gave back nothing: from attention on, TensorE was busy at half clock for 25.8 us in the first layer before and for 38.3 after (summed over windows of half a microsecond), 6 us more lost. Ahead of attention some of it came back, so that over the whole stage 2.6 and 0.8 us a layer were lost where 7.5 were to be gained. "Two thirds come back with the waits" was wrong: more and shorter waits had no fewer half-clock stretches behind them.

**Part 5 (-4.8) had the right mechanism and was low in cost.** The date of bank 6 gave a loss of 3.6 us a place to the first product against 4.7 forecast in block 1, and 24 products in 5.62 us are the price forecast. In block 2 the first product is 1.6 and 1.9 us later after FFN and mixer, but the 1.6 comes with the new FFN end, not with the products. The clock came up in full behind the FFNs (1.00) and nearly behind the mixers (0.86), not by half. By the first products and a clock in full that would be some -3, and yet leaving the products out brought 10 by traces and 16 by medians, the forecast's lower bound. The step that failed is the credit for the clock, 4.8: I took what the clock gives right behind the turns as a gain of the span. The windows there came up, but block 2's mixers take 465.9 and 462.4 us without the products and 466.0 and 464.3 with them: against the 20 products' own 4.7 us stand 2.5 and 2.8 us less idle time, and 3.0 and 0.3 from the clock. Of the traces' 10, 6.7 are the two places behind block 1's mixer and 1.4 those behind block 2's.

**The sum.** The parts as measured are 21, 7, 7, 19 and -16, which add up to the 38 of the whole. They mix medians with stages of single executions and leave out the mixers' ends, so that they fit so well is in part luck. The tenth taken off for new waits, 8 us, was far too little: parts 2, 4 and 5 fell short by 17, 37 and 11.

**Rivals.** A (3280) had the size of part 4 nearly right (25, measured 19), but its mechanism, VectorE as the limit, was true of one wait only; B had the unread products free, and they cost 16; D (3271) had the wrong cause. The prediction has A with part 2's low end outside its range, but 3280 + 12 is 3292, inside; it takes part 5's low end as well to get to 3303. No rival had half clock that stays while idle time goes.

**Signs named in advance.** No last-rows wait over 0.5 us: seen. None at attention's first turn, and mixers of block 2 shorter by 25 to 30 us: neither (3.61 us, and 2.8 and 4.5). L2129 free of a wait for GpSimd: seen. The first turn after block 1's mixers 4 to 5 us later: seen (10.5 us after the last rows in place of 5.9). Of the signs of being wrong, low-split waits and residual operations of 5 us came.

**Still open:** why the old order of block 2's mixer takes 476 us in the new surroundings and 469 in the old. The later first product is 1.5 of it and a wait of 4.69 in place of 2.65 at the decay product 2 more. By the three terms, the 7.1 us of the first layer are 4.3 of work and 3.6 of half clock less 0.7 of idle time, and the 6.8 of the second 5.1, 0.5 and 1.2. The work is the unread products' 4.7 us. What isn't explained is why the idle time doesn't fall by what they fill. Open too is what decides between 0.64 and 1.00 behind the same wait.

## What to carry to other kernels

Before an edit moves the victim of a wait away, ask what else will stand there: a held port or a full engine takes the next operation, so mend the holder (shorter instructions on GpSimd brought 18 us in the changed kernel, most of it half clock, but 6 in the kernel before, where a second cause stood in front of the same wait) and charge a wait for an engine without gaps as moved in full. Filling an idle stretch with unread products needs a target that is free when the stretch begins; the same products cost 16 us in one bank and brought 10 in another, in the kernel where everything else was mended. The worth of an edit is read by undoing it alone, not from the change of its stage. And idle time and half clock are to be kept apart in such a reading: the idle time of four mends added up (20.8 us), their half clock did not (35.5 against 19.5).

## What the runs showed of the hardware

- The same product behind the same wait of 2.05 us had a window at 0.64 behind it in one kernel and one at 1.00 in another. So the same mixer with 45 to 46.5 us of idle time took between 457 and 466 us a layer: of the 8.5 us 7.3 are half clock (34.3 us busy at it, or 49.0) and 1.2 idle time. And edits in block 1 moved block 2 by up to 7 us a layer.
- In the 12 us from the last rows, at eight places in the kernel, the granted clock was 0.62 to 0.72 without unread products, 1.00 or 0.86 with them in a bank that comes free late, and 1.00 with them in one that is free in time. The Trainium skill ("TensorE: Matmul & The Clock Gate", Part 4: PE-mode transpose) has transposes not counting as busy for the clock in the same way; the traces fit that (0.57 behind block 2's FFN with 16 transposes), but don't test it alone, since TensorE also idles for 4.29 and 1.66 us among them.
- A GpSimd operation of 4.52 us held a VectorE operation on two columns for 4.19; as four pieces (5.0 us together) it held it for 0.91.
